# A gated-delta scan with modulation matmuls woven in: three modulation turns move from TensorE pieces to VectorE steps

## The reference

```python
# block 1
c_act = silu(c)
mod = c_act @ w_ada + b_ada                  # w_ada: 2048 x 12288
sh1, sc1, gt1, sh2, sc2, gt2 = split(mod, 6)
h = rmsnorm(x) * (1 + sc1) + sh1
p = h @ w_in
y = concat(rwkv7_mixer(p[..., :n]), pool_mixer(p[..., n:]))
x = x + gt1 * (y @ w_out)
h = rmsnorm(x) * (1 + sc2) + sh2
x = x + gt2 * conv_ffn(h)
# inside rwkv7_mixer, for each of 16 heads and each token t:
S = S * w_t + (S @ a_t) b_t^T + v_t k_t^T
y_t = S @ r_t
# block 2: latent attention and dilated attention, with a modulation of its own (2048 x 6144)
```

## Time and profile before

| | us |
|---|---|
| median of 3 runs (2654.91 to 2656.66) | 2655.5 |
| profiled execution | 2664.16 |
| its span | 2662.3 |
| TensorE matmul busy | 2578.9 |
| VectorE busy | 1877.7 |
| ScalarE busy | 1097.0 |
| GpSimd busy | 413.3 |

### The profile page before, as it was taken

The page is one execution under the profiler, slowest core; times in us unless marked ns, Lnnn a source line. Parts: engine busy times, 40 slices in busy tenths (PEclk is TensorE's granted clock), DMA queues, the critical chain, the costliest instruction groups (busy, mean ns, idle before and its releaser), DMA issues.

```text
span 2662.3 us, 41991 instructions
## 1 busy us (share of the span) xinstructions
PE 2578.9 (97%) x18000; PEld 2238.7 (84%) x18000; DVE 1877.7 (71%) x2469; ACT 1097.0 (41%) x1312; POOL 413.3 (16%) x272
## 2 busy tenths in 40 slices
PE   6899999999999999999999999999999999999997
PEld 3678877788888888888889999999888888889996
DVE  2238753277999999999987777776547875886554
ACT  2253322244433443434455544444434444444453
POOL 0047111021000000000020677760000000000001
PEclk8899999799999999999999999999999999999998
DMA  9958477876898888888955887875766656666663
GB/s 341 340 168 229 124 242 246 260 201 179 233 273 260 262 259 261 253 267 253 269 177 133 225 214 219 224 202 175 190 194 178 168 165 189 175 159 174 190 187 114
DMA packets 744921, 570.21 MB, mean 214 GB/s; under 512 B 44544, under 2 KB 629376, under 8 KB 744608
## 3 DMA queue, kind: packets, MB, share of 16 engines
q1 hardware_dynamic: 744736, 567.52, 73.2%
HBM read 565.38 MB, written 2.10 MB: 213 GB/s over the span
## 4 chain that ended last, share of the span: by engine, by line
PE 78%; DVE 13%; DMA 4%; issue 2%; ACT 2%; POOL 1%; SPq 0%; DVEq 0%; POOLq 0%
PE bank L865 28%; PE bank L868 14%; PE bank L832 4%; DVE w_low L1951 4%; PE bank L833 3%; PE bank L834 3%; PE bank L1118 2%; PE bank L821 2%; PE bank L1270 2%; PE bank L1271 2%; PE bank L1272 2%; DMA ring<-w_up 2%; PE bank L903 2%; PE bank L902 2%; PE bank L901 2%
## 5 line engine op out<-in xcount | busy, mean ns | idle before, releaser
L1951 DVE TENSOR_TENSOR w_low<-ring,w_high 128x2048 fp32r<-128x2048 f32 (+1 forms) x389 | 891.6, 2294 | 331.0 <-ACT w_high L1489 324.5
L865 PE MATMUL bank<-acts,w_high 128*128 128x512 f32 x4128 | 993.4, 393 | 1.6 <-ACT vd L1902 1.6
L1489 ACT ACTIVATE w_high<-ring 128x2048 fp32r<-128x2048 f32 (+1 forms) x389 | 738.7, 1901 | 429.3 <-DMA ring<-w_up 186.4
L865 PEld LDWEIGHTS bank<-acts,w_high 128*128 128x128 f32 x4128 | 759.9, 189 | 152.4 <-issue 2.8
L868 PEld LDWEIGHTS bank<-acts,w_low 128*128 128x128 f32 x4128 | 529.2, 191 | 21.0 <-DVE w_low L1951 1.0
L868 PE MATMUL bank<-acts,w_low 128*128 128x256 f32 x4128 | 535.6, 283 | 0.5 <-DVE w_low L1951 0.5
L769 POOL TENSOR_SCALAR prod_g<-adg,cact 128x512 f32<-128x512 f32 x60 | 121.6, 2027 | 64.4 <-DMA adg<-w_ada 61.1
L1270 PE MATMUL bank<-w_high,hid_high 128*128 128x512 f32 x320 | 125.2, 391 | 2.9 <-DVE w_low L1951 2.9
L1271 PE MATMUL bank<-w_low,hid_high 128*128 128x512 f32 x320 | 124.7, 390 | 0.0
L1272 PE MATMUL bank<-w_high,hid_low 128*128 128x512 f32 x320 | 124.5, 389 | 0.0
L691 POOL TENSOR_TENSOR sumf<-sqf 128x256 f32<-128x256 f32 x1 | 0.7, 742 | 781.2 <-ACT sqf L1932 781.2
(11 more groups left out here) (470 smaller groups left out, 3512.8 us busy)
## 6 DMA issues: line engine op xcount, KB each, us to landing
ring<-w_in SPq DMA_DIRECT2D x176, 1024.0 KB, 5.8
ring<-w_up SPq DMA_DIRECT2D x88, 1024.0 KB, 8.2
ada<-w_ada SPq DMA_DIRECT2D x76, 1024.0 KB, 6.8
adf<-w_ada SPq DMA_DIRECT2D x48, 1024.0 KB, 5.2
ring<-w_down SPq DMA_DIRECT2D x44, 1024.0 KB, 6.8
ring<-w_out SPq DMA_DIRECT2D x16, 1024.0 KB, 5.9
adg<-w_ada SPq DMA_DIRECT2D x64, 256.0 KB, 5.5
ring<-w_mla SPq DMA_DIRECT2D x16, 1024.0 KB, 5.7
```

Source lines behind the costliest of these rows:

```text
L865: pe.matmul(o, wh[:, j], both, start=j == 0, stop=False, skip_group_check=True)
L1489: act.activation(WH[s][:, 0:WIDE[n]], ring[s][:, 0:WIDE[n]], ACT.Copy).then_inc(high_done, 1)
L1951: v.tensor_tensor(WL[s][:, 0:WIDE[n]], ring[s][:, 0:WIDE[n]], f32(WH[s][:, 0:WIDE[n]]), ALU.subtract)\
```

## The change

Eleven turns stood in the scan as TensorE pieces. Three of them (numbers 16, 17 and 18) become eighths on VectorE: 24 eighths of two steps each, into accumulators `acc_s` 0 to 2. N_EARLY goes from 19 to 16, so that 8 turns, 40 pieces, stay in TensorE's order. Taken out are: the first piece of a level in levels 1 to 3 of the first half and 0 to 3 of the second, and in every chunk the piece behind YS and the one behind the first parts of S and Y. `ada` now sums `acc_s` and `acc_e`, 16 one-column matmuls, behind chunk 2 and not behind chunk 0.

VectorE does eighths behind evictions: one behind M35 in each half, one behind each level (two from level 1 on in the first half), two behind Z in chunks 0 to 2, one behind y in chunks 0 and 1. SyncE issues their loads between the piece loads: two behind the fourth piece load, and each further one three piece loads ahead of what its buffer's last user stood at. The reload of `xT` now waits for the sums behind chunk 2.

```diff
+def level_pieces(tt, lv):
+    return 2 if lv == 4 or (tt, lv) == (0, 0) else 1
+def eighths_behind(where, tt, at=0):
+    return {"masks": 1, "level": 2 if tt == 0 and at > 0 else 1, "Z": 2, "Y": 1}[where]
+def eighth_loads():
...
+    for k in range(2, len(eighths)):
+        p = eighths[k - 2]
+        p = p // 5 * 4 + min(p % 5, 4)
+        behind.setdefault(p + 3, []).append(k)
+    return {p: len(ks) for p, ks in behind.items()}, len(eighths)
...
+        acc_s = [at(f"acc_s{k}", 10 + 2 * k, [P, 512]) for k in range(3)]
...
-        N_EARLY, N_FIRST, N_TURNS, N_FFN, N_LATE = 8 + 11, 1, 12, 11, 4
-        FIRST_TURNS = ((0, 16 + 3),)
-        AFTER = 8 + 4
+        N_EARLY, N_POOL, N_FIRST, N_TURNS, N_FFN, N_LATE = 8 + 8, 1, 4, 12, 11, 4
+        FIRST_TURNS = ((0, 19), (0, 16), (0, 17), (0, 18))
+        AFTER = 8 + 6
...
-            for t in range(N_EARLY - 9):
-                ada_rows(w_ada, 2 * D + 512 * t)
+            for p in range(4 * (N_EARLY - 9)):
+                ada_rows(w_ada, 2 * D + 512 * (p // 4), (p % 4,))
+                if p == 3:
+                    first_turns(2)
+                first_turns(EIGHTHS.get(p, 0))
...
-                    mod_piece()
+                    if level_pieces(tt, lv) == 2:
+                        mod_piece()
...
-                    mod_piece()
                     os, oy = k_bank(tt, "S", c), k_bank(tt, "Y", c)
...
-                    mod_piece()
                     for hb in range(2):
                         in_sbuf(tt, "Z", c, hb)
...
-                    if n == 0:
-                        ada(acc_e)
+                    if n == 2:
+                        ada(*acc_s, acc_e)
...
+            def eighths(n):
+                for _ in range(n):
+                    first = B.up("eighth") - 1
+                    turn, eighth = divmod(first, 8)
+                    k = 8 * N_POOL + first
+                    if first == 0:
+                        v.wait_ge(ada_sums, N_POOL)
+                    v.wait_ge(f_landed[k % 2], 16 * (k // 2 + 1))
+                    acc = acc_s[turn][:, :]
+                    for j in range(2):
...
+                        if eighth == j == 0:
+                            seq(v.tensor_scalar(acc, w, col, None, ALU.mult))
+                        elif j == 0:
+                            seq(v.scalar_tensor_tensor(acc, w, col, acc, ALU.mult, ALU.add))
+                        else:
+                            v.scalar_tensor_tensor(acc, w, col, acc, ALU.mult, ALU.add).then_inc(f_free, 1)
+                            v.wait_ge(f_free, k + 1)
...
+                eighths(eighths_behind("masks", tt))
...
+                    eighths(eighths_behind("level", tt, lv))
...
+                    if n < 3:
+                        eighths(eighths_behind("Z", tt))
...
-                    if n == 0:
+                    if n < 2:
+                        eighths(eighths_behind("Y", tt))
+                    elif n == 2:
                         v.wait_ge(ada_full, AFTER + 1)
-                        v.tensor_copy(mod[:, 76:80], bank[6][:, 0:4]).then_inc(ada_free, 1)
+                        v.tensor_copy(mod[:, 64:80], bank[6][:, 0:16]).then_inc(ada_free, 1)
```

More of the change, by code:

```diff
@@ L35 @@
 LEVELS = (1, 2, 4, 8, 16, 32)
+def level_pieces(tt, lv):
[3 more added lines that the diff above has]
+def eighth_loads():
+    pieces, eighths = [], []
+    for tt in range(2):
+        pieces += ["piece"] * 4
+        eighths += [len(pieces)] * eighths_behind("masks", tt)
+        for lv in range(5):
+            pieces += ["piece"] * level_pieces(tt, lv)
+            eighths += [len(pieces)] * eighths_behind("level", tt, lv)
+        pieces += ["piece"] * (2 - tt)
+        for c in range(2 - tt):
+            eighths += [len(pieces)] * eighths_behind("Z", tt)
+            pieces += ["piece"] * 2
+            if tt == 0:
+                eighths += [len(pieces)] * eighths_behind("Y", tt)
+    behind = {}
+    for k in range(2, len(eighths)):
[3 more added lines that the diff above has]
+    return {p: len(ks) for p, ks in behind.items()}, len(eighths)
+EIGHTHS, N_EIGHTHS = eighth_loads()
 WINDOWS = (2, 4, 8, 16)
@@ L713, in _ @@
             k = 0
-            for t, (block, _) in enumerate(FIRST_TURNS):
+            for block, _ in FIRST_TURNS[:N_POOL]:
                 for eighth in range(8):
@@ L1633, in _ @@
                 mod_piece(2)
-                for n in LEVELS[1:]:
+                for lv, n in enumerate(LEVELS[1:]):
                     for hb in range(2):
@@ L1637, in _ @@
                         act.activation(T1[:, hb, :, :], o[:, :], ACT.Copy).then_inc(f, 1)
-                    mod_piece(2)
+                    mod_piece(level_pieces(tt, lv))
                 if tt == 0:
@@ L2212, in heads @@
                 return t.rearrange("p (a b) -> p a b", a=n)
+            def eighths(n):
[8 more added lines that the diff above has]
+                    for j in range(2):
+                        col = cact[:, 2 * eighth + j:2 * eighth + j + 1]
+                        w = AE[k % 2][:, 512 * j:512 * j + 512]
+                        if eighth == j == 0:
[5 more added lines that the diff above has]
+                            v.wait_ge(f_free, k + 1)
+                    if eighth == 7:
+                        v.memset(small[:, 59:60], 0.0).then_inc(ada_sums, 1)
             LOW, LOWT = 2, 8
```

## The result

The changed kernel takes 2662.8 us in the median of ten executions (2658.1 to 2673.1), the kernel before 2655.9 beside it (2652.3 to 2660.7). The ratio is 1.0033, with a 95% interval of 1.0018 to 1.0048: slower by a third of a per cent, where 9 us less were forecast. The profiled execution of after took 2659.9 us, at the low end of its ten; the one of before, 2664.2, was above all of its ten. So the two spans can't be set against each other, and what follows compares the scan, from its first woven piece to the token sums behind it: 179.3 us before, 182.8 after, by the starts in TensorE's timeline. That is 3.5 us of the 7 between the medians. The ratio's interval is 5 to 13 us. One profile of each doesn't say where the rest lies: behind the scan TensorE has the same program in all kernels here, and that part took between 2132.0 and 2141.7 us in their profiles.

The account below looks back on a forecast made before the run. TensorE, busy for 97% of the span, was taken to bound the kernel. The terms -15.0 + 2.9 + 0.5 + 0 + 0 + 2.9 gave -8.7, say -9, from 2655.5: 2646.5 us, range 2637 to 2657.

Parts of the forecast that it names:

- Term 1: 15 TensorE pieces fewer in levels and chunks, 1.00 us each at the full clock, nothing exposed: -15.0 us.
- Term 6: TensorE's clock in chunks and sums: the low clock costs 14 us in place of 11.1, +2.9 us.
- worse clock: Thinned chunks fall to 1.2 GHz and stay, each giving 10.1 us back; ends slower from 2.25 chunks; chance 0.18.
- Term 3: VectorE's 24 eighths in the scan, hidden by its waits for TensorE: +0.5 us, between 0 and 3.
- Term 2: Column sums: four accumulators behind the third chunk, 3.84 us, where one took 0.96 behind the first: +2.9 us.
- Term 4: Scan loads, now 24 half-megabytes in two buffers, cost 0, with up to 8 us kept for a rival.
- late eighths: Eighths' loads landing at 7 to 8 us put VectorE behind in four levels and second chunk: +5 to +8; chance 0.12.
- Term 5: The tail, with the first w_out load, moves with the scan: 0, between -1 and +2 us.

Follow-up runs that it names:

- before_thin: The kernel before with the scan's piece loads cut to 256 KB each, all 55 pieces in place: 2650.3 us, ratio 0.9969.
- thin_loads: The changed kernel with each piece's and each eighth's load in the scan cut to 256 KB: 2638.7 us, ratio 0.9929.
- more_loads: The kernel before with 24 half-megabyte loads that nobody reads issued between its piece loads, TensorE's program unchanged: 2663.9 us, ratio 1.0037.
- thin_no_steps: thin_loads with VectorE's eighths emptied, only the first step of each turn left: 2636.4 us, ratio 0.9936.
- thin_dense: thin_loads with up to 16 unneeded matmuls of 64 columns at each of the 15 places of removed pieces: 2654.5 us, ratio 1.0006.
- fill_coarse: The changed kernel with four unneeded matmuls of 512 columns at each of the 15 places of removed pieces: 2663.4 us, ratio 1.0028.

## Why the prediction was wrong, step by step

**Term 1 failed: "nothing is exposed, the full microsecond is gained".** Each place was asked which eviction the piece covers, and that answer holds: no wait on T appears, and an undisturbed level takes 6.74 us. Not asked was what else a piece covers. It holds TensorE for a microsecond with 8 matmul records, where small products use up 64 in two microseconds. An undisturbed level has 200 matmuls in 6.74 us, 127 in 4.3; before, with a piece more, 208 in 7.88, 127 in 4.8. A block of instructions is needed that much sooner, beside loads that hold up the start of its packet. The pauses are 10.5 us, 9.7 more than before.

**Term 6: the size in the chunks was near, its place and cause were wrong.** The four chunks took 14.60, 11.16, 10.61 (485.70 to 496.31) and 17.77 us, 54.1 against four undisturbed ones of 10.07, so 13.9 lost where I had said 13 for the chunks, 1.6 of it pauses. But the levels, which I had at 2.4 GHz throughout, fell twice, and the clock's cost is counted there too. The fall was attributed to thinner work; before_thin and thin_loads, 13.7 us low both, say that thinning alone does nothing. In after three of the falls come in or just behind a pause. That pauses cause them is argued, not shown: more_loads has 7.1 us of pauses and is low for 6.8 us, thin_no_steps has 0.6 and is low for 27.3. The rival "worse clock" had the right sign for another reason: one chunk was low throughout, not the 2.25 that it needed. Together: 13.7 us more at the low clock. In the last chunk the low clock cost 17.77 - 10.07 = 7.7 us in 17.8, 0.43 for each; by that, an estimate, 5.9 us. 9.7 + 5.9 = 15.6, and the scan is off from the sum without its clock term by 3.5 + 11.6 = 15.1. With low-clock times that vary by more than 10 us between executions, that these two meet so closely is luck.

**Terms 1 to 3 under quiet supply were sized right.** -15.0 + 2.9 + 0.5 = -11.6, and thin_loads against before_thin is -11.6. That this meets to the tenth is luck: the intervals of the two ratios are 10 and 7 us wide, and by the ratios the difference is -10.6, by the profiled scans -10.9. The wait for S of 3.9 us is not in the sum either; something else must make up for it.

**Term 3's bound was mis-sized.** The row that I took (1.07 us against 0.43 beside GpSimd) gave a factor of 2.5; the step of 0.75 us went to 2.27 to 2.74, a factor of 3 to 3.7, and it was four steps in a row, on the one eviction that the next chunk needs. The cover was said to hold 0.4 us of it for an eighth; a single step went over by 1.5 to 2.0. It costs nothing in after only because TensorE is late itself.

**Term 2 held but for the clock.** The sums, L844 of after, take 4.38 us from 496.31 to 500.69 where 3.84 was said; the granted clock in them was 0.81.

**Term 4 held.** A landing of ade took 3.7, 5.8 and 13.6 us (least, median, most), longer at worst than the 8.0 of the earlier trace rows, and still no eighth waited for its load over 0.61 us. The rival "late eighths" falls. (The slack that the prediction set against late loads there, 1.4 us, is not the 0.6 + 1.1 of its term 3; the 0 doesn't depend on it.)

**Term 5 held.** The first w_out load is issued at 519.05 and split at 528.07, 9.0 us later, as in the earlier trace rows.

```profile
519.05 5.17 SPq L520 DMA_DIRECT2D ring<-w_out  x2
```
```profile
528.07 1.91 ACT L1528 ACTIVATE w_high<-ring 128x2048 fp32r<-128x2048 f32 x1 [1.87 <-DMA ring<-w_out]
```

**Shown and argued.** Shown: what is late is a block of instructions (all 79 pauses end 1.2 to 1.7 us after a packet of 16 KB has landed on the instruction queue, at the same matmul numbers in different kernels). The pauses come of dense matmuls and traffic together: thin_dense has the first alone and no pause, fewer loads take them away in after and in before (but for one of 0.6 us in thin_no_steps), more_loads makes them with an unchanged program, and at like traffic before and fill_coarse have fewer than after. And the change is worth some -11 us without them. Argued: that the pauses make the clock fall. Open: why a packet starts later beside more traffic and why two loads in flight change nothing, why more_loads is slower as a whole, and some 3 us of the difference between the medians that the two scans don't hold.

## What to carry to other kernels

When a large instruction is taken out from among small ones, ask three things of its place: which eviction it covers, which transfer, and how much sooner the engine will want its next instructions. The last shows as idle time with the releaser "issue" inside a group of like instructions; look in the trace for an instruction packet that lands just before each hole ends, count the instructions between two such holes, and see whether the holes go when the loads beside them are cut. And take one profile of the kernel before with its loads cut as well: it says at once whether a gain on paper is lost to the transfers.

## What the hardware showed that was not expected

- TensorE pauses of 0.2 to 2.7 us in after, one, two or three times about 126 matmuls apart, in stretches with small matmuls beside 123 to 325 GB/s of loads; none at 98 GB/s (thin_loads) or 90 (thin_dense), one of 0.6 us in thin_no_steps. Each ends 1.2 to 1.7 us after a 16 KB packet of instructions has landed, and such a packet takes about 1 us.
- The clock fell to 1.2 GHz in or behind such pauses, ended at 386.12, 408.08 and 462.37, and at 499.1, within one-column matmuls that kept TensorE busy for 4.38 us; with 15 pieces fewer and no pauses it was low for the same 13.7 us as with them all. The Trainium skill, TensorE: Matmul & The Clock Gate, "Why this matters for your kernels", names idle gaps as what throws the clock back. Three of the four falls here come with a gap, though the gaps, of 1.4 to 2.7 us, are shorter than those that the page speaks of; the one in the busy one-column sums doesn't agree.
- A VectorE step on two SBUF operands of 128x512 takes 2.27 to 2.74 us beside GpSimd's bonus, 0.75 alone. The GpSimd operations beside it take 2.22 to 2.69 us.
